# All low parts of the expert weights subtracted on VectorE

## What is computed

```python
def swiglu(x, wg, wu, wd):
    return (jax.nn.silu(x @ wg) * (x @ wu)) @ wd
...
    for e in range(N_EXPERTS):
        out = out + gate[:, e:e + 1] * swiglu(xt, wg[e], wu[e], wd[e]).astype(jnp.float32)
```

## Time and profile before

| | |
|---|---|
| median of 3 runs | 1764.94 us (1764.79 to 1766.91) |
| the profiled execution | 1761.52 us, its span 1759.7 us |
| mean granted TensorE clock | 0.929 of 2.4 GHz |
| TensorE (PE) busy | 1555.0 us, 88% of the span |
| VectorE (DVE) busy | 1153.0 us, 66% |
| ScalarE (ACT) busy | 813.4 us, 46% |
| GpSimd (POOL) busy | 828.7 us, 47% |
| read from HBM | 254.54 MB, 150 GB/s over the span |

### The profile page before, as it was taken

The page is one execution under the profiler, slowest core; times in us unless marked ns, Lnnn a source line. Parts: engine busy times, 40 slices in busy tenths (PEclk is TensorE's granted clock), DMA queues, the critical chain, the costliest instruction groups (busy, mean ns, idle before and its releaser), DMA issues.

```text
span 1759.7 us, 22898 instructions
## 1 busy us (share of the span) xinstructions
PE 1555.0 (88%) x8707; PEld 1361.5 (77%) x8707; DVE 1153.0 (66%) x1564; ACT 813.4 (46%) x1352; POOL 828.7 (47%) x414
## 2 busy tenths in 40 slices
PE   7798888899799999688988898888999899899885
PEld 6687787787699999567888788765878778778774
DVE  6779786557611011686979844855787688688774
ACT  4544443532333243353534434322666566567653
POOL 4457565426376667343756642440343244234332
PEclk9999899989899999898998997996999999999987
DMA  5222223312355453322222332233687588588771
GB/s 230 96 96 75 70 72 101 144 48 90 121 165 160 130 159 106 123 72 96 77 85 81 95 127 72 72 133 114 217 324 291 199 308 304 200 301 306 262 253 41
DMA packets 57523, 264.66 MB, mean 150 GB/s; under 512 B 9024, under 2 KB 9664, under 8 KB 48448
## 3 DMA queue, kind: packets, MB, share of 16 engines
q1 hardware_dynamic: 57408, 263.11, 43.3%
HBM read 254.54 MB, written 8.54 MB: 150 GB/s over the span
## 4 chain that ended last, share of the span: by engine, by line
PE 47%; DVE 29%; POOL 10%; issue 9%; ACT 4%; DMA 1%; POOLq 0%; ACTq 0%; DVEq 0%; SPq 0%
POOL fl L528 7%; PE ps L1320 6%; PE ps L1321 6%; PE ps L1322 6%; DVE cacc L1565 6%; PE ps L1025 5%; PE ps L1026 4%; PE ps L1027 4%; PE ps L1293 3%; DVE ml L1907 2%; DVE kT L1473 2%; DVE qT L1473 2%; DVE pw L1538 1%; DVE G L1810 1%; POOL ml L592 1%
## 5 line engine op out<-in xcount | busy, mean ns | idle before, releaser
L548 POOL TENSOR_TENSOR Wl<-raw,Wh 128x1024 fp32r<-128x1024 f32 x138 | 344.5, 2500 | 351.3 <-ACT Wh L619 351.0
L1025 PE MATMUL ps<-Xh,Wl 128*128 128x320 f32 x976 | 335.0, 343 | 49.1 <-POOL Wl L548 31.4
L1907 DVE TENSOR_TENSOR ml<-mraw,mh 128x1408 fp32r<-128x1408 f32 (+1 forms) x160 | 299.4, 1892 | 105.1 <-ACT mh L910 104.5
L592 POOL TENSOR_TENSOR ml<-mraw,mh 128x1408 fp32r<-128x1408 f32 (+1 forms) x56 | 184.9, 3302 | 363.5 <-ACT mh L910 363.5
L910 ACT ACTIVATE mh<-mraw 128x1408 fp32r<-128x1408 f32 (+1 forms) x216 | 268.4, 1252 | 112.5 <-PE ps L1322 109.1
L1026 PE MATMUL ps<-Xl,Wh 128*128 128x320 f32 x976 | 314.1, 322 | 0.0
L1027 PE MATMUL ps<-Xh,Wh 128*128 128x320 f32 x976 | 313.8, 322 | 0.0
L1025 PEld LDWEIGHTS ps<-Xh,Wl 128*128 128x128 f32 x976 | 195.5, 200 | 76.3 <-POOL Wl L548 43.1
L528 POOL TENSOR_TENSOR fl<-fraw,fh 128x1024 fp32r<-128x1024 f32 (+1 forms) x60 | 158.8, 2652 | 88.2 <-ACT fh L857 88.2
L1026 PEld LDWEIGHTS ps<-Xl,Wh 128*128 128x128 f32 x976 | 195.6, 200 | 0.3
L1027 PEld LDWEIGHTS ps<-Xh,Wh 128*128 128x128 f32 x976 | 194.6, 199 | 0.0
(11 more groups left out here) (336 smaller groups left out, 3151.7 us busy)
## 6 DMA issues: line engine op xcount, KB each, us to landing
mraw<-w_moe SPq DMA_DIRECT2D x128, 704.0 KB, 6.3
raw<-w_mix SPq DMA_DIRECT2D x68, 1024.0 KB, 4.9
mraw<-w_moe SPq DMA_DIRECT2D x88, 512.0 KB, 4.3
fraw<-w_ffn SPq DMA_DIRECT2D x44, 512.0 KB, 3.5
fraw<-w_ffn SPq DMA_DIRECT2D x16, 704.0 KB, 4.0
Ss<-st_delta SPq DMA_DIRECT2D x2, 2048.0 KB, 9.1
o_delta_s<-Ss SPq DMA_DIRECT2D x8, 512.0 KB, 2.6
X<-x SPq DMA_DIRECT2D x2, 640.0 KB, 5.7
```

The costliest lines, as they stand in the source:

```text
L548: pool.tensor_tensor(Wl[:, n % 3, :], raw[:, b % 3, u % 2, :], Wh[:, n % 3, :].bitcast(f32), ALU.subtract).then_inc(w_lo, 1)
L592: pool.tensor_tensor(ml[:, n % MS, 0:w], mraw[:, n % MRAW, 0:w], mh[:, n % MS, 0:w].bitcast(f32), ALU.subtract).then_inc(m_lop, 1)
L1025: pe.matmul(out, wl, xh, start=start, stop=False)
L1907: dve.tensor_tensor(ml[:, n % MS, 0:w], mraw[:, n % MRAW, 0:w], mh[:, n % MS, 0:w].bitcast(f32), ALU.subtract).then_inc(m_lod, 1)
```

## The change

The list of units whose low part GpSimd makes is emptied. `pooled` is then false for every n: GpSimd's loop in the expert stage makes nothing, VectorE makes all 216 low parts, and `m_rest` counts on VectorE's semaphore alone.

```diff
--- before.py
+++ after.py
@@ -52,7 +52,7 @@
 MT = NE * MN
 MRAW, MS = 7, 4
 SCAT = 3
-MPOOL = (3, 6, 9, 12, 19, 22, 25)
+MPOOL = ()
```

## The result

Four runs of the changed kernel took 1735.56 to 1739.01 us, median 1736.64. Four runs of the kernel before had a median of 1765.93. The ratio is 0.9834, with a 95% interval of 0.9811 to 0.9858. The forecast was 1740, the range 1727 to 1750. A second set of runs gave 1735.88 us and 0.9837 (0.9820 to 0.9853). The profiled execution took 1735.56 us against 1761.52.

A forecast was written before the change was run, and what follows sets the result against it. TensorE, 88% busy, was taken to bound the kernel, losing time to stops and a lower clock. Gains of 2.6 + 1.3 + 12 + 9 = 25 us from a median of 1764.9 gave 1740 us, range 1727 to 1750.

The forecast's parts named there:

- The bound: Expert stage: TensorE alone near full, 88% busy; overlapping low parts of VectorE and GpSimd wait for each other, stopping TensorE.
- (1): GpSimd's expert loop: 56 low parts removed, 184.9 us of its time, no gain by itself.
- (2): VectorE: 77 us of low parts added, 70 us and 17 us taken off in return; load about even.
- (3): Preamble: six places no longer wait for GpSimd's unit 3, so the gathers start earlier; 2.6 us.
- (4): Unit 3 of later experts: TensorE's 0.18 us wait goes, VectorE done with 0.8 us cover; 1.3 us.
- (5): TensorE's stop before the L1358 transposes: falls to 1.85 us in experts 1 to 7 but does not vanish; 12 us.
- (6): TensorE's clock around the seven stops: five falls stay, 13 of 22 us, so 9 us are gained.
- A: Rival: TensorE's idle time shrinks but every fall of the clock stays; 1749 us, chance 0.18.
- B: Rival: no fall of TensorE's clock is left after the stops; 1727 us, chance 0.22.
- C: Rival: VectorE becomes the bound, slower, decided from 1.85 us per wide low part on; 1780 us, chance 0.04.
- D: Rival: no effect, as ScalarE or transfers set TensorE's stops; chance 0.04.

The follow-up runs named there:

- The runs with the scratch tile: Changed kernel, but GpSimd subtracts or copies constants into a scratch tile that nobody reads: 1807.63 us with the subtraction, 1756.98 us with the copy.
- The run with the addition first: Changed kernel with the eighth addition put ahead of VectorE's low part of unit 13: 1721.60 us, ratio 0.9726 to the kernel before.
- the kernel with units 3, 6 and 9: Changed kernel with the low parts of units 3, 6 and 9 given back to GpSimd: 1757.64 us, ratio 0.9939 to the kernel before.
- the kernel with the zeros: Changed kernel, but GpSimd writes zeros into a scratch tile that nobody reads: 1735.90 us, ratio 0.9829 to the kernel before.

## Why the prediction was right

**The bound.** Two instructions that overlap were read as waiting for each other, from one pair 1.49 us apart. The runs with the scratch tile confirm it with 1.48 us and without any shared data. A pair on a timeline carried more than all means.

**(1), (2), the load.** VectorE's even load came out as worked: 1153.0 to 1146.9 us. The undisturbed durations are 1.62 and 1.22 us.

**(3), the preamble.** 2.6 us forecast, 5.69 - 3.08 = 2.61 measured.

**(4), unit 3.** TensorE waits for no low part, so the cover held and 1.3 us came. In expert 3 VectorE is done with unit 3 at 1412.8 us (1411.28 and its 1.54), and TensorE starts it at 1413.66, 0.8 us later as worked out.

**(5), the stop.** Forecast 1.85 us in all seven, measured 1.89; waits of 13 us forecast, 13.2 measured. That it would not vanish was the step most open to doubt, and it rests on asking what is late next: ScalarE's SiLU, and then VectorE's own order, in which the new low part of unit 12 stands ahead of two additions. The run with the addition first shows that order was the cause.

**(6), the clock.** The mis-sized term, and a guess. I took five falls at 2.6 us, so 13 of 22 us would stay; four stayed, mostly short, 8.6 us. The term was 9 and measured 13.4, and with 1.7 for a fall in the last expert that I had not counted it is more than the 4 us by which the gain (29 us in the runs) came out above the forecast of 25. That five was near four is luck rather than reading: the two rows behind it decide nothing. The 1.87 us of idle time with a fall are two stops, 0.78 and 1.08 us, and behind the window with one stop of 2.17 us and no fall came a second stop, 2.61 us up to 913.51, with a fall between 914 and 916 us. The two cases A and B were the right ends: with 0.67 us stops one fall in seven is left, with none no fall, with 2.36 us or more all seven. A stop of 1.89 us lies between. What decides for one expert and not for the next stays open: with the down units on GpSimd stops of the same length had a fall five times, and with the seven units on GpSimd and unit 11 in front, four of five stops of 1.16 us had a fall behind them.

**The rivals.** C (VectorE becomes the bound) failed on its point of decision: a wide low part needs 1.62 us, not 1.85. But the run with GpSimd's subtraction kept comes near to what C describes, the full load on VectorE with slow low parts: there a wide low part takes 1.98 us in the mean, and the time is 1808 us, more than C's 1780. The Trainium skill, Perfetto Trace Analysis, section "Optimizing Scalar/DVE Operations", warns that moving work between these two engines may not help because of the port; here the split cost 29 us, and undoing it left VectorE no busier (1153.0 to 1146.9 us). D failed with the stops.

## What to carry to other kernels

Before work is shared between VectorE and GpSimd, look in the two timelines for instructions that overlap: if the later one ends its own full length after the earlier one, the later one waited for the earlier. Here such a split took nothing off VectorE, since an overlap could cost it two of its own low parts; where VectorE had time to spare, in the down matrix, it cost nothing either. When a stop of TensorE goes, ask what is late next, in which engine's order and by how much, and price the clock apart, as a term with both ends. A wait that remains can be covered by moving one independent piece of the waiting engine's own work in front of it, here one unit of matmuls.

## What was new about the hardware

- A GpSimd instruction that reads keeps a two-input VectorE instruction waiting even where they share no tile, with one input or two; one that only writes zeros does not (56 memsets of 0.95 to 1.29 us, no low part above 1.63 us). A one-input tensor_scalar of VectorE waited even for those, up to 1.40 us instead of 0.28, in four groups of places.
- GpSimd's copy of 128x1408 float32 takes 1.36 us, a subtraction of two tiles 3.24, and one whose two inputs are the same tile 2.53.
- The waiting goes both ways: GpSimd's subtraction took 4.39 us when VectorE came first (the kernel with units 3, 6 and 9), and ended 3.10 us after VectorE's low part.
- The clock after a stop of TensorE that small matmuls follow: no stop, no fall in seven; 0.67 us, one; 1.87 to 1.90 us, four in the changed kernel in both of its profiles, five with the down units on GpSimd; 1.89 to 2.15 us (the kernel with the zeros), five; 2.36 us and more, all seven. The length is not all: with GpSimd in use and the stop covered in part, four of five stops of only 1.16 us were followed by a fall. Why these fell more often than stops of 1.89 us was not settled.
